# One spread of gate products goes from step 6 to step 8 of a head pair, and the first norm's row is computed after the small tables

## The reference

```
h = rms_norm(x, g_mix)
z = h @ w_in                       # q | k | v (3 groups x 8 heads x 64) | u (512) | gate_a | gate_s (1024 each)
a = dilated_attention(q, k, v)     # 3 window/dilation groups, q and k normed per head, causal
y = gelu(s5_ssm(u, ...))           # 32 groups of 16 channels, 64 complex states each
s_out = (y @ w_glu_a) * sigmoid(y @ w_glu_b)
mix = sigmoid(gate_a) * (a @ w_attn_proj) + sigmoid(gate_s) * s_out
x = x + mix @ w_out
h2 = rms_norm(x, g_ffn)
x = x + (silu(h2 @ w_ffn_gate) * (h2 @ w_ffn_up)) @ w_ffn_down
```

## Time and profile before

| | |
|---|---|
| median of 3 runs | 861.52 us (861.45 to 862.01) |
| the profiled execution | 861.43 us, of which the trace's span is 859.6 |
| PE busy | 849.0 us, 99% of the span |
| DVE, ACT, POOL busy | 571.9, 361.0, 249.0 us |
| TensorE's granted clock | full (2.4 GHz) in all 40 slices |
| chain that ended last | 89% PE, 7% DVE, 1% each ACT, DMA, POOL |
| line 1555 in that chain | 43% |
| line 1075 (DVE) in that chain | 2% |

### The profile page before, as it was taken

How to read it: one execution, slowest core, us unless ns; L and a number is a source line. 1 busy time by engine, 2 the same in 40 slices (tenths; PEclk the granted TensorE clock), 3 DMA queues, 4 the chain that set the end, 5 groups by cost and what they waited for, 6 DMA issues and landing times.

```text
span 859.6 us, 15077 instructions
## 1 busy us (share of the span) xinstructions
PE 849.0 (99%) x5171; PEld 728.8 (85%) x5171; DVE 571.9 (67%) x790; ACT 361.0 (42%) x575; POOL 249.0 (29%) x266
## 2 busy tenths in 40 slices
PE   9999999999999999999999999999999999999998
PEld 7888778888888778887887888889999999888886
DVE  6458985567934554645587565889999999533334
ACT  6312343323345656746433443344454454222221
POOL 0689985010020000001220220057566675000000
PEclk9999999999999999999999999999999999999999
DMA  8439238534465543413645233323333333322222
GB/s 311 146 111 233 74 123 176 185 113 137 137 219 164 166 130 111 149 59 91 154 141 185 86 98 98 99 74 98 98 110 110 114 105 102 109 92 95 95 71 98
DMA packets 103494, 108.87 MB, mean 127 GB/s; under 512 B 11712, under 2 KB 69296, under 8 KB 103328
## 3 DMA queue, kind: packets, MB, share of 16 engines
q1 hardware_dynamic: 96544, 94.25, 35.6%
q10 hardware_dynamic: 5504, 10.52, 3.8%
q0 software_dynamic: 1408, 3.61, 1.9%
HBM read 94.38 MB, written 13.96 MB: 126 GB/s over the span
## 4 chain that ended last, share of the span: by engine, by line
PE 89%; DVE 7%; ACT 1%; DMA 1%; issue 1%; POOL 1%; SPq 0%; ACTq 0%; DVEq 0%; POOLq 0%
PE ps L1555 43%; PE ps L1870 18%; PE ps L1890 13%; PE ps L1832 6%; DVE early L1075 2%; PE ps L1750 2%; PE ps L1779 1%; PE ps L1735 1%; PE ps L1721 1%; DVE w_lo L660 1%; PE ps L1725 1%; DMA early<-in_xt 1%; DVE late L1537 1%; DVE w_lo L1427 1%; DVE h_lo L1423 1%
## 5 line engine op out<-in xcount | busy, mean ns | idle before, releaser
L660 DVE TENSOR_TENSOR w_lo<-w_raw,w_hi 128x1024 fp32r<-128x1024 f32 x109 | 139.5, 1280 | 208.2 <-ACT w_hi L654 208.1
L654 ACT ACTIVATE w_hi<-w_raw 128x1024 fp32r<-128x1024 f32 x109 | 115.4, 1059 | 281.5 <-PE ps L1555 165.3
L1555 PE MATMUL ps<-w_hi,hT_hi 128*128 128x512 f32 x280 | 109.6, 392 | 0.6 <-DVE early L993 0.4
L1555 PE MATMUL ps<-w_lo,hT_hi 128*128 128x512 f32 x280 | 109.0, 389 | 0.0
L1555 PE MATMUL ps<-w_hi,hT_lo 128*128 128x512 f32 x280 | 109.0, 389 | 0.0
L1555 PE MATMUL ps<-hT_hi,w_hi 128*128 128x512 f32 x224 | 91.4, 408 | 0.0
L1555 PE MATMUL ps<-hT_hi,w_lo 128*128 128x512 f32 x224 | 87.7, 391 | 0.0
L1555 PE MATMUL ps<-hT_lo,w_hi 128*128 128x512 f32 x224 | 87.4, 390 | 0.0
L498 POOL TENSOR_TENSOR early<-early 128x16 f32<-128x16 f32 (+5 forms) x125 | 77.8, 622 | 10.1 <-ACT early L714 0.4
L1870 PE MATMUL ps<-h_hi,w_hi 128*128 128x256 f32 x256 | 72.9, 285 | 0.6 <-DVE w_lo L1427 0.5
L1870 PE MATMUL ps<-h_lo,w_hi 128*128 128x256 f32 x256 | 72.4, 283 | 0.0
(11 more groups left out here) (249 smaller groups left out, 1788.1 us busy)
## 6 DMA issues: line engine op xcount, KB each, us to landing
w_raw<-in_w_in SPq DMA_DIRECT2D x108, 256.0 KB, 3.7
w_raw<-in_w_ffn_down SPq DMA_DIRECT2D x44, 256.0 KB, 2.9
w_raw<-in_w_ffn_gate SPq DMA_DIRECT2D x64, 128.0 KB, 2.2
w_raw<-in_w_ffn_up SPq DMA_DIRECT2D x64, 128.0 KB, 2.4
z_d<-early ACTq DMA_DIRECT2D x7, 1024.0 KB, 4.8
late<-z_d SPq DMA_DIRECT2D x96, 64.0 KB
w_raw<-in_w_out SPq DMA_DIRECT2D x16, 256.0 KB, 3.1
late<-z_d SPq DMA_DIRECT2D x12, 256.0 KB
```

Source lines behind the costliest of these rows:

```text
L654: nc.scalar.activation(w_hi[:, j % WSPL], w_raw[:, j % WRAW], ACT.Copy).then_inc(w_hi_done, 1)
L660: nc.vector.tensor_tensor(w_lo[:, j % WSPL], w_raw[:, j % WRAW], w_hi[:, j % WSPL].bitcast(F32), ALU.subtract).then_inc(w_lo_done, 1)
L1555: ins = T.matmul(ps[:, bank0 + m], lhsT, rhs, start=first and h == 0 and k == 0, stop=last and h == 1 and k == 2)
```

## The change

Two edits, independent of each other. The norm's row on DVE goes from between the angle tables and the denominator tables to behind the last table, directly ahead of `lo(W_U, 0)`. And in PE's table of gate steps one step goes from `u` = 6 to `u` = 8: step 6 has one instead of two, and step 8 one instead of none.

```
@@ vector
             tab(V.tensor_scalar(sv[RR], sv[RR], PI_BELOW, -PI_BELOW, ALU.min, ALU.max))
-            dve.wait_ge(norm_sums, 1)
-            V.tensor_scalar(norm_row[:, :], ps[:, 6, 0:2 * TB].rearrange("p (n e) -> p n e", e=2)[:, :, 0], 1.0 / DM, EPS,
-                            ALU.mult, ALU.add).then_inc(norm_eps, 1)
             tab(V.tensor_tensor(sv[DEN], sv[LR], sv[LR], ALU.mult))
...
             V.tensor_tensor(dadd, eye16[:, :].unsqueeze(1).to_broadcast([P, 4, CH]),
                             dsk.unsqueeze(2).to_broadcast([P, 4, CH]), ALU.mult).then_inc(dve_tab, 1)
+            dve.wait_ge(norm_sums, 1)
+            V.tensor_scalar(norm_row[:, :], ps[:, 6, 0:2 * TB].rearrange("p (n e) -> p n e", e=2)[:, :, 0], 1.0 / DM, EPS,
+                            ALU.mult, ALU.add).then_inc(norm_eps, 1)
             lo(W_U, 0)
@@ tensor, in the loop over u
-                        for _ in range((1, 1, 1, 2, 1, 1, 2, 1, 0, 1)[u]):
+                        for _ in range((1, 1, 1, 2, 1, 1, 1, 1, 1, 1)[u]):
                             next(gates)
```

## The result

The changed kernel takes 857.31 us (median of 5, 856.82 to 857.92) against 861.60 for the kernel before beside it: half a per cent less (ratio 0.9949, 95% interval 0.9937 to 0.996). The forecast was 857.3. The profiled execution went from 861.43 to 857.08 us.

The account below looks back on a forecast made before the run. PE, busy for 99% of the span, bounds the kernel. Profiled 861.43 - 2.9 (gate steps) - 1.3 (POOL's shift) = 857.2, with the median 0.09 above, so 857.3; own range 856.6 to 858.2 (chance 0.62), wider range 856.4 to 860.0.

Parts of the forecast that it names:

- The gate steps: Gate step moved from step 6 to 8: values 0.74 us earlier per pair, taken as 0.72 x 4 = 2.9 us.
- The arrivals: PE in one pair: turn 5 at 278.13, charged to 278.19, turn 6 at 279.91, turn 7 at 281.63, values at 283.44.
- the 0.06 that I charged for nothing: Turn 5 on PE: 0.06 us allowed for the transposes' weights not being loaded ahead.
- a tie: Turn 5 arrives on PE at 278.13 and copy 4 on ACT releases PE at 278.12.
- The row's price at its place: First norm: DVE's row starts 1.43 us later, at 26.01, and costs PE 0.
- The held power: POOL's power near 26 us: ends at 27.35, or 28.3 if held by `lo(W_U, 0)`; POOL 0.27 or some 1.2 us later.
- POOL's shift: POOL's lag takes wide operations out of DVE's gaps before line 1651: -1.3 us, bounds a gain of 1.6, a loss of 0.9.
- The two prices of 0.86 and 0.84: Time DVE's `lo` at 114.66 and last table product lose to 512-wide POOL operations running at their front.
- the side effect on the wait for line 993: 128-element POOL operations lengthen DVE's product at 94.52 by 0.2 or 0.3; PE's wait of 0.4 rises to 0.6 or 0.7.
- That lag stays as work not done: POOL runs its table chain almost without pause for another hundred microseconds, so its lag near 26 us persists to 112 us.
- later by only the 0.28: POOL at 112 us: a lag of 0.28 would put a copy in the gap at 114.66, and one 0.8 would be gone.
- a loss of 0.9 if a third 512-wide operation slips in: Lower bound of POOL's part: a third 512-wide operation ahead of DVE's last table product costs 0.9 us.

Follow-up runs that it names:

- The step to 7: Changed kernel with the gate step put at step 7 instead of step 8, turn 7 again directly behind turn 6: 860.10 us (ratio 0.9978).
- the experiment where it starts first: Kernel before with the norm's row only behind the reciprocal, so POOL's power starts ahead of `lo(W_U, 0)`: 861.82 us (ratio 0.9995).
- the kernel with the row alone: Kernel before with only the norm's row moved behind the small tables, gate steps as before: 860.45 us (ratio 0.998).
- one product more: Kernel before with a single unused 16-wide product added on POOL behind the power: 861.76 us (ratio 0.9996).
- POOL early: Changed kernel with three memsets of POOL's table chain moved ahead of its wait for the norm's row: 862.34 us (ratio 1.0008).
- more work on an engine that PE does not wait for: Kernel before with four more unused 16-wide products on POOL behind the power: 861.01 us (ratio 0.9989).

## Why the prediction was right, and where it wasn't

**The gate steps.** Forecast 0.74 per pair, charged at 0.72; measured 7.54 - 6.75 = 0.79 in pair 0, and 0.78 from pair to pair (the earlier trace rows and the table above). The arrivals hold to 0.05: turn 5 came 1.50 after the gate step (1.49, plus the 0.06 that I charged for nothing), the others 1.71 and 1.72 apart, the values 1.82 behind turn 7 (1.81). Taking each copy's start from ACT's own order was right: copies 5 and 6 start behind exp 6 and exp 7. But that turn 5 doesn't wait was in part luck. Copy 4 starts at 276.11 and by the lag of 0.55 releases PE at 276.66, 0.04 before turn 5; the forecast called it a tie. The step to 7 shows that the reason was the right one.

**The row's price at its place.** Zero on PE, as forecast: ACT's and DVE's first evacuations slipped to 28.34, and no wait of PE is near. The row came at 26.14, 0.13 later than worked out; the whole start was 0.12 later.

**The held power.** Both bounds had been left open; the upper one was right, by the power's 1.86 us here and 1.02 in the experiment where it starts first. With the Trainium skill's rule of an exclusive lock between VectorE and GpSimd ("SBUF — State Buffer", "SBUF: two separate sides") only half of that agrees. The power was held as long as the remainder ran, as the rule has it. But the rule gives the pair to whoever starts first for the whole instruction, and in the experiment the power, started 0.28 us first and running until 27.18, did not hold the remainder, which started at 26.44 and took its undisturbed 1.22. For the power the measurement decides: it does not hold DVE for its whole length.

**POOL's shift.** Forecast 1.3 by way of DVE, measured 1.39 at line 1651, and 1.41 from the sums of squares on in the kernel with the row alone. The 1.3 was a choice between wide bounds (a gain of 1.6, a loss of 0.9), so that it came this close is partly luck. The two prices of 0.86 and 0.84 were right (0.84 and 0.85 came back), and so was the size of the side effect on the wait for line 993 (0.2 to 0.3, measured 0.28). Its place was not: the product at 94.52 takes 2.56 in both kernels, and it is the remainder ahead of it that went from 1.23 to 1.48. Two more statements of that part were wrong. "That lag stays as work not done" is false: an operation that waits for DVE takes up a lag in its waiting time, and the changed kernel's own lag fell from 0.99 us to 0.50 by 45 us. So "later by only the 0.28" was not enough, as one product more showed; the forecast held because the power was held too, which the rows had left open. And the lower bound, "a loss of 0.9 if a third 512-wide operation slips in", holds at most for a POOL that is late: with POOL early five DVE instructions are held by 512-wide operations, and PE's clock falls in the longer wait.

**Sum.** 2.9 + 1.3 = 4.2 forecast; 3.2 (4.58 - 1.39) in the pairs and 1.4 before them, less 0.2 of a wait elsewhere, 4.35 measured by the profiled executions and 4.3 by the medians. The pairs gave 0.3 more than forecast, and the wait near 436 us took 0.2 of it back.

## What to carry to other kernels

Where two short operations use one PSUM bank in turn and each has to be copied out, put a piece of independent work between them: it is worth the wait and the restart, 0.79 us here for a listed wait of 0.58. Where DVE and POOL both run long chains, look at which POOL operation stands in each gap of DVE's critical chain; a shift of POOL by a microsecond far ahead can be worth more than the instruction that was moved, in either direction. Such a gain hangs on a coincidence, so it would be better to fix what makes it (keep wide POOL operations out of that stretch) than to rely on it; that was not tried here.

## What the runs showed of the hardware that I had not expected

A 512-wide POOL operation ahead of a DVE instruction with two inputs costs even a small one most of a microsecond: two of 32 elements took 0.93 us instead of 0.19 and 0.23 behind operations that run 1.06 and 1.09. A power on POOL of only 4 elements per partition takes 1.02 us; held up, it still needs 0.88 once DVE is done, and while it runs DVE is not held (a remainder took 1.22 us beside it). And more work on an engine that PE does not wait for in that stretch made the kernel faster by 1.0 us (0.3 to 1.7 by the interval's ends of the ratio).
